# Down products of two MLPs: stretches of two sets of terms instead of three

## The reference, cut to what matters

```python
# first block, D_FF = 2816
x = x + (silu(h @ w_gate) * (h @ w_up)) @ w_down
# second block, D_FF_2 = 4096
x = x + square(relu(h @ w_up)) @ w_down
```

## Time and profile before

| | us |
|---|---|
| median of three runs | 3051.46 |
| the profiled execution | 3051.11 |
| its span, first to last instruction | 3049.3 |
| PE busy | 2893.5 (95%) |
| DVE busy | 2035.0 (67%) |
| POOL busy | 1704.2 (56%) |
| ACT busy | 1323.4 (43%) |
| down products of `mlp1`, PE's stretch | 1416.7 to 1667.4 |
| down products of `mlp2`, PE's stretch | 2704.5 to 3034.8 |

### The profile page before, as it was taken

The page is one execution under the profiler, slowest core; times in us unless marked ns, Lnnn a source line. Parts: engine busy times, 40 slices in busy tenths (PEclk is TensorE's granted clock), DMA queues, the critical chain, the costliest instruction groups (busy, mean ns, idle before and its releaser), DMA issues. The chain is left out here.

```text
span 3049.3 us, 38594 instructions
## 1 busy us (share of the span) xinstructions
PE 2893.5 (95%) x13868; PEld 2226.8 (73%) x13868; DVE 2035.0 (67%) x3107; ACT 1323.4 (43%) x2088; POOL 1704.2 (56%) x1202
## 2 busy tenths in 40 slices
PE   7999999999999999999897999998999999999998
PEld 5666666667788788887786666666778788877876
DVE  5677886875232777778678555567662688887667
ACT  4455553555433333334344344456563433344332
POOL 5533324222344899999887211132103799988885
PEclk8999999999999999999998999999999999999999
DMA  6312212111351233334441311010002254454433
GB/s 186 87 49 55 57 49 56 56 42 56 112 171 54 87 102 103 103 103 163 169 148 38 116 34 34 18 45 18 11 4 97 87 158 151 152 197 169 153 126 104
DMA packets 264989, 283.92 MB, mean 93 GB/s; under 512 B 25525, under 2 KB 226101, under 8 KB 264245
## 3 DMA queue, kind: packets, MB, share of 16 engines
q1 hardware_dynamic: 264824, 281.84, 29.6%
HBM read 195.00 MB, written 76.84 MB: 89 GB/s over the span
## 5 line engine op out<-in xcount | busy, mean ns | idle before, releaser
L2537 POOL TENSOR_TENSOR w_lo<-w_raw,w_hi 128x512 fp32r<-128x512 f32 x166 | 228.8, 1399 | 459.4 <-ACT w_hi L1454 459.4
L1053 PE MATMUL big<-g_hi,w_hi 128*128 128x512 f32 (+1 forms) x1248 | 417.1, 415 | 20.4 <-POOL w_lo L2537 8.6
L1053 PE MATMUL big<-g_lo,w_hi 128*128 128x512 f32 (+1 forms) x1248 | 389.8, 394 | 0.0
L1053 PE MATMUL big<-g_hi,w_lo 128*128 128x512 f32 (+1 forms) x1248 | 388.4, 393 | 0.0
L1053 PEld LDWEIGHTS big<-g_hi,w_hi 128*128 128x128 f32 (+1 forms) x1248 | 213.7, 189 | 144.1 <-issue 100.7
L1053 PEld LDWEIGHTS big<-g_hi,w_lo 128*128 128x128 f32 (+1 forms) x1248 | 234.7, 188 | 52.7
L1053 PEld LDWEIGHTS big<-g_lo,w_hi 128*128 128x128 f32 (+1 forms) x1248 | 234.0, 188 | 52.2
L1479 ACT ACTIVATE a_hi<-a_raw 128x512 fp32r<-128x512 f32 x114 | 72.1, 633 | 407.0 <-POOL a_raw L2545 406.4
L1739 ACT ACTIVATE d_hi<-d_sum 128x384 fp32r<-128x384 f32 (+2 forms) x123 | 59.7, 486 | 328.4 <-POOL d_sum L2677 328.4
L2553 POOL TENSOR_TENSOR a_lo<-a_raw,a_hi 128x512 fp32r<-128x512 f32 x114 | 180.4, 1582 | 31.9 <-ACT a_hi L1479 31.1
L1335 PE MATMUL big<-b_hi,a_hi 128*128 128x512 f32 x456 | 178.0, 390 | 5.2 <-POOL a_lo L2553 3.0
(11 more groups left out here) (415 smaller groups left out, 7721.3 us busy)
## 6 DMA issues: line engine op xcount, KB each, us to landing
set_raw<-op_spill SPq DMA_DIRECT2D x54, 512.0 KB, 4.6
w_raw<-in_w_in SPq DMA_DIRECT2D x51, 512.0 KB, 4.3
d_raw<-in_w_down SPq DMA_DIRECT2D x60, 384.0 KB, 4.0
op_spill<-c SPq DMA_DIRECT2D x43, 512.0 KB, 2.7
set_raw<-op_spill SPq DMA_DIRECT2D x27, 768.0 KB, 6.2
w_raw<-in_w_up SPq DMA_DIRECT2D x27, 512.0 KB, 5.9
u_raw<-in_w_up SPq DMA_DIRECT2D x27, 512.0 KB, 5.3
op_spill<-op_t_mlp SPq DMA_DIRECT2D x25, 512.0 KB, 3.7
```

What stands on the lines that cost most here:

```text
L1053: ins = pe.matmul(out[0:m, HALF * h:HALF * h + HALF], w[slot][:, col:col + m], x[:, HALF * h:HALF * h + HALF], start=p == 0, stop=p == tot ...
L2537: ins = pool.tensor_tensor(w_lo[s][:, half], w_raw[s][:, half], w_hi[s][:, half].bitcast(F32), ALU.subtract)
```

## The change

One line of `windows`. Before, the jobs took turns in threes: at t = 0, 3, 6, ... job 0, at t = 1, 4, ... jobs 3 and 1, at t = 2, 5, ... job 2, and each then covered the three sets since its last turn. After, jobs 0 and 3 take turns with jobs 1 and 2, so two stretches stand at each t and each covers two sets. At the last t all four jobs finish with what is left.

```diff
-            for job in FINISH[stage] if last else {0: (0,), 1: (3, 1), 2: (2,)}[t % 3]:
+            for job in FINISH[stage] if last else ((0, 3), (1, 2))[t % 2]:
```

## The result

The changed kernel took 3112.04 us (median of 3 runs, 3111.79 to 3112.94) against 3051.46 before: a ratio of 1.0203, 95% interval [1.0189, 1.0217], so +60.6 us. The forecast was +37.4 (3088.5), its range ended at 3112. The direction was right, POOL is the bound as forecast, and the size was 23 us short.

What follows compares the result with a forecast made beforehand. POOL bounds the kernel, PE right beneath. Fronts +24.3 (mlp1) and +26.3 (mlp2), tails -9.2 and -4.0, sum +37.4 us on 3051.1: 3088.5 us. Own range 3076 to 3102; 8-in-10 range 3067 to 3112.

Steps and rivals of the forecast that it cites:

- A clean two-set stretch: POOL's two-set stretch without a set's load, from its first row to the next stretch: 8.95 us.
- DVE's 170 adds fit: DVE in the steady part: busy 53.2 of 62.7 us with the added adds, fitting unless it must idle over 9.5 us.
- both tails get shorter: After the first job's end, DVE becomes the bound: -9.2 us in mlp1 and -4.0 us in mlp2.
- ACT's and SP's added instructions cost nothing: ACT's 119 instructions, some 23 us of issue at under half load, and the added weight DMAs were costed at nothing.
- the disturbed stretch is now shorter, which saves 0.6 a load: POOL's stretches beside a set's load: price 3.0 instead of 3.6 us, -4.3 us in mlp1 and -7.3 us in mlp2.
- well off 11.9: Sign of being wrong: POOL's loaded two-set stretches differing clearly from the forecast 11.9 us.
- Forming and starts as before: Stage starts and last operands' forming: no extra term for their stalls, which were taken to be in POOL's sum.
- the landing that the prediction named beside the one-set stretches: Weights landing in about 4 us beside 5.65 us stretches: if that fails, a microsecond or two four times; costed at nothing.
- a set is asked for one stretch earlier: Set transfers requested one stretch earlier relative to first use; DMAs were costed at nothing.
- The lag: PE ends about 4.3 us behind POOL at the end of the fronts, taken as unchanged.
- The fourth rival: PE's clock falls behind idle gaps: at mean 0.88 a set needs 21.6 us on PE, +15, 3103 us; chance 0.04.

Runs made afterwards that it cites:

- e1: Kernel before, six of seven d_lo of every three-set stretch issued on POOL as two instructions over the same elements; 1.0087 of before, +27 us.
- e4: Changed kernel, three of seven d_lo of most two-set stretches made for one set instead of two; 1.0058 of before, 44 us less than the changed kernel.
- e5: Changed kernel, position 6's d_lo made by DVE instead of POOL except in a stage's first and last four stretches; 1.0145 of before, -18 us against changed.
- e2: Kernel before with 135 more DVE instructions, banks copied onto themselves behind adds of three-set stretches; 1.0013 of before, +4 us.
- e3: Changed kernel without three of the ten DVE adds of a stretch, from the fifth stretch on except a stage's last four; 1.0223 of before.
- e10: Changed kernel with the last operand's spill on SP behind the next stretch's loads instead of ahead of a set's load; 1.0182 of before.
- e13: Kernel before, from the third set on low parts are a copy by ACT, not DVE's subtraction, ACT's pieces behind positions 0, 1, 3; 0.9914 of before.
- e11: Changed kernel with only ACT's three roundings of a set moved behind its positions 0, 1 and 3 instead of 1, 2 and 3; 1.0189 of before.
- e9: Changed kernel, low parts copied by ACT instead of DVE's subtraction, ACT's pieces behind positions 0, 1, 3; 1.0004 of before, -61 us against changed.
- e14: Changed kernel, but mlp1 starts as before, then jobs 2 and 0 alternate with 3 and 1, one stretch less in mlp1; 1.0170 of before.
- e6: Kernel before with position 6's d_lo made by DVE instead of POOL; 0.9984 of before, -5 us.
- e8: Changed kernel, from the third set on low parts are a copy by ACT, not DVE's subtraction, pieces behind positions 1, 2, 3; 1.0125 of before.

## Why the prediction was short

**Right.** POOL is the bound (e1, e4, e5). A clean two-set stretch is 8.95, and 0.14 us of each POOL instruction is not its elements (e1; the earlier trace rows give 0.18). DVE's 170 adds fit (e2, e3, e4); both tails get shorter. That ACT's and SP's added instructions cost nothing by themselves was not tested alone.

**The term that failed: "the disturbed stretch is now shorter, which saves 0.6 a load".** It took 4.3 and 7.3 us off. The price of a load stayed at 3.6, and twelve loaded stretches of seventeen were "well off 11.9", the prediction's own sign of being wrong. What POOL loses to a load is most of the length of DVE's three pieces (3.3 of 1.2 + 1.2 + 1.7 us above) and half a microsecond of waiting for ACT, and neither shrinks with POOL's stretch. The two loads that the 3.0 rested on the earlier trace rows were those in which a piece fell on a wait; in the steady run that is one load in three. The 17 loads took 213.5 us where 11.93 each make 202.8: 10.7 us. With the price of the three-set stretches, a set would have come to 8.95 + 12.6 = 21.5; 21.6 was measured (2821.45 to 3015.49 for nine sets).

**Left at nothing, and worth 14.5 us.** "Forming and starts as before": POOL's second to fourth stretches took 3.8 us more than by the forecast's prices in `mlp1` and 4.8 in `mlp2`. In `mlp1` POOL waited 1.4 there for PE; in `mlp2` ACT waited 3.8 and POOL 1.2 for a stretch's weights, the landing that the prediction named beside the one-set stretches and left out of the sum. What then remains of the fronts, 5.0 and 0.9, lies mostly in the forming stretches. Of it, 2.6 were SP's order (e10): "a set is asked for one stretch earlier" did not hold for the one behind the spill. It is the same DVE that forms and makes `set_lo` there (e13).

**The lag.** At the end of the fronts PE stood 6.5 and 6.3 us behind POOL, not 4.3: +2.2 and +1.9. The fourth rival was put at 0.04 because before's steady part showed a clock of 1.00 beside its short gaps; the changed kernel's waits are longer, and behind them the clock fell (0.88 in the 14 us above). Its sum, 21.6 us a set at a mean clock of 0.88, happens to be the period measured, but not by its path: at the 0.96 measured in `mlp2`'s front, PE's 19.04 would be 19.8, and from 2800 to 3025 POOL waited for PE not once. The fall cost little by itself, since POOL and not PE was the bound; in e11, where PE was, it cost what POOL had gained.

**The tails.** They gave more: measured to DVE's last add, -14.1 and -6.3 instead of -9.2 and -4.0. The tail of before in `mlp1` holds 8 pairs, not 9.

The sum, in the profiled executions: 37.4 + 10.7 + 14.5 + 4.1 - 7.2, and 1.5 for what lies around the stages, is 61.0, the difference of the spans. That POOL's period sets the stage was right; the price of a load was wrong in its mechanism, and forming and starts, put at nothing, were not nothing. That these terms add up is my accounting of one execution; shown by experiment are the parts that e4, e9 with e13, e10 and e14 moved. Whether the 0.6 saved a load would come in a plan whose pieces always meet a wait was not tried.

## What to carry to other kernels

A price per event that was read in one phase (two loads at the start) belongs to the way in which the two engines met there; in a steady run take it from how long the disturber works, and count a wait that covers it only as often as it occurs. When a mean period lies just above another engine's, look at how many stretches really waited before pricing a relief: in the kernel before, four of thirteen did (e6). And work that reaches into the bound engine can be taken away (e9) and still be replaced by an in-order queue's delay (e8): in these two runs, both without true low parts, a few positions in ACT's order were worth 37 us.

## What the runs showed of the hardware

- A DVE subtraction with both inputs in SBUF holds a POOL instruction for up to nearly its own length: 0.74 became 1.78 beside 1.23 us of DVE, 2.29 beside 1.75, and 0.93 beside 0.46. DVE's adds with one input in PSUM do not (POOL 0.74 beside a row of them), nor do ACT's copies (0.74 in e8). It goes the other way too: the DVE piece of 1.52 us above, elsewhere 1.23, began while POOL's row of 2889.60 still ran. The Trainium skill, "SBUF — State Buffer", SBUF: two separate sides, calls the pair of ports that VectorE and GpSimd share an exclusive lock: whoever starts first has it for the whole instruction, and the other is blocked. The trace agrees, with the numbers above. That the price of a load hangs on DVE's length and not on POOL's stretch follows from it, and the 3.6 us before and after the change bear it out.
- PE's waits cost twice: behind 2.45 us without a matmul in the changed kernel, and 2.77 in e11, the next matmuls started 0.43 us apart instead of 0.23, before they came back to 0.23.
- A POOL subtraction over 128x384 split in two parts costs 0.14 us more than whole.
